# Weight buffers of an fp32r kernel: one tensor per slot, six offsets within 512 bytes

## What is computed

```python
for l in range(2):
    proj = rms_norm(x, norm_mix[l]) @ w_in[l]          # 1024 x 5120
    ...
    x = x + mixed @ w_out[l]                           # 1024 x 1024
    up = rms_norm(x, norm_ffn[l]) @ w_up[l]            # 1024 x 5632
    x = x + (silu(conv(up[..., :2816])) * up[..., 2816:]) @ w_down[l]
proj = rmsnorm(x, norm_mix_w) @ w_in_2                 # 1024 x 3080
...
x = x + mix @ w_out_2
u = relu(rmsnorm(x, norm_mlp_w) @ w_ff1)               # 1024 x 4096
x = x + (u * u) @ w_ff2
return rmsnorm(x, final_norm_w)
```

## Time and profile before

| | |
|---|---|
| median of three runs | 1057.65 us (1056.1 to 1057.9) |
| profiled execution | 1055.63 us |
| its span, first to last instruction | 1053.9 us |
| mean granted TensorE clock | 0.998 of 2.4 GHz |
| instructions | 20016 |

### The profile page before, as it was taken

How to read it: one execution, slowest core, us unless ns; L and a number is a source line. 1 busy time by engine, 2 the same in 40 slices (tenths; PEclk the granted TensorE clock), 3 DMA queues, 4 the chain that set the end, 5 groups by cost and what they waited for, 6 DMA issues and landing times.

```text
span 1053.9 us, 20016 instructions
## 1 busy us (share of the span) xinstructions
PE 1039.0 (99%) x8398; PEld 984.3 (93%) x8398; DVE 720.2 (68%) x1217; ACT 572.9 (54%) x791; POOL 287.1 (27%) x179
## 2 busy tenths in 40 slices
PE   8999999999999999999999999999899999999997
PEld 7999998999999899999999989998899999899996
DVE  5762248887687775322878967877887779666663
ACT  6454466655355645445665635566548865343443
POOL 0376665100000137666640000013300035101120
PEclk9999999999999999999999999999999999999999
DMA  9644445565654764444456576446432157664841
GB/s 310 200 161 150 160 162 160 160 219 162 223 197 126 223 212 160 137 148 153 158 166 208 160 233 201 143 139 220 121 117 86 61 181 229 190 210 129 260 162 40
DMA packets 169705, 180.11 MB, mean 171 GB/s; under 512 B 4240, under 2 KB 166416, under 8 KB 169488
## 3 DMA queue, kind: packets, MB, share of 16 engines
q1 hardware_dynamic: 169616, 178.84, 53.0%
HBM read 177.78 MB, written 1.05 MB: 170 GB/s over the span
## 4 chain that ended last, share of the span: by engine, by line
PE 84%; DVE 7%; ACT 4%; POOL 2%; issue 2%; DMA 1%; SPq 0%; POOLq 0%; ACTq 0%; DVEq 0%
PE psum L679 83%; DVE sb_w_lo L1861 2%; POOL sb_w_lo L2614 1%; ACT sb_scratch L1329 1%; ACT sb_w_hi L1329 1%; DVE sb_xg_lo L1845 1%; DVE psum L1845 1%; POOL sb_scratch L2654 1%; DMA sb_raw<-in_w_ff 1%; DMA sb_raw<-in_w_in 1%; PE psum L906 1%; DVE sb_hid_both L1936 0%; DVE sb_xt L1879 0%; DVE sb_scratch L1845 0%; DVE sb_xt L1877 0%
## 5 line engine op out<-in xcount | busy, mean ns | idle before, releaser
L1329 ACT ACTIVATE sb_w_hi<-sb_raw 128x2048 fp32r<-128x2048 f32 (+3 forms) x185 | 318.4, 1726 | 163.5 <-PE psum L679 99.0
L679 PE MATMUL psum<-sb_xg_hi,sb_w_hi 128*128 128x256 f32 x1656 | 401.8, 283 | 0.1
L679 PE MATMUL psum<-sb_xg_lo,sb_w_hi 128*128 128x256 f32 x1656 | 396.7, 279 | 0.0
L1861 DVE TENSOR_TENSOR sb_w_lo<-sb_raw,sb_w_hi 128x2048 fp32r<-128x2048 f32 (+3 forms) x150 | 305.9, 2042 | 104.7 <-ACT sb_w_hi L1329 103.8
L679 PEld LDWEIGHTS psum<-sb_xg_hi,sb_w_hi 128*128 128x128 f32 x1656 | 310.3, 187 | 3.3 <-DVE sb_xg_lo L1845 0.8
L679 PEld LDWEIGHTS psum<-sb_xg_lo,sb_w_hi 128*128 128x128 f32 x1656 | 310.7, 188 | 0.3
L679 PE MATMUL psum<-sb_xg_hi,sb_w_lo 128*128 128x256 f32 x1656 | 228.3, 280 | 0.1
L679 PE MATMUL psum<-sb_hid_both,sb_w_hi 128*128 128x512 f32 (+1 forms) x912 | 210.5, 364 | 1.3 <-DVE sb_xt L1874 0.6
L679 PEld LDWEIGHTS psum<-sb_xg_hi,sb_w_lo 128*128 128x128 f32 x1656 | 207.9, 187 | 1.0 <-DVE sb_w_lo L1861 0.3
L2614 POOL TENSOR_TENSOR sb_w_lo<-sb_raw,sb_w_hi 128x2048 fp32r<-128x2048 f32 (+1 forms) x34 | 156.0, 4595 | 107.3 <-ACT sb_w_hi L1329 97.9
L679 PEld LDWEIGHTS psum<-sb_hid_both,sb_w_hi 128*128 128x128 f32 x912 | 148.7, 188 | 23.0 <-DVE sb_hid_both L1936 1.2
(11 more groups left out here) (172 smaller groups left out, 987.3 us busy)
## 6 DMA issues: line engine op xcount, KB each, us to landing
sb_raw<-in_w_in SPq DMA_DIRECT2D x51, 1024.0 KB, 5.3
sb_raw<-in_w_up SPq DMA_DIRECT2D x44, 1024.0 KB, 5.1
sb_raw<-in_w_ff SPq DMA_DIRECT2D x21, 1024.0 KB, 5.7
sb_raw<-in_w_down SPq DMA_DIRECT2D x16, 768.0 KB, 4.8
sb_raw<-in_w_down SPq DMA_DIRECT2D x16, 640.0 KB, 4.4
sb_raw<-in_w_out SPq DMA_DIRECT2D x8, 1024.0 KB, 5.2
sb_raw<-in_w_ff SPq DMA_DIRECT2D x8, 768.0 KB, 4.5
sb_raw<-in_w_ff SPq DMA_DIRECT2D x8, 640.0 KB, 4.5
```

The source lines that it names most:

```text
L679: return nc.tensor.matmul(ps, lhsT, rhs, start=start, stop=stop, skip_group_check=True)
L1329: return nc.scalar.activation(out_, in_, func, **kw)
L1861: v.tensor_tensor(part(w_lo, s), part(raw, s), part(w_hi, s).bitcast(F32), ALU.subtract)\
```

## The change

The three tensors become nine, one for each slot and part, and five small tensors that nothing uses lie between them: before `w_hi1` 72 columns, before `w_hi2` 16, before `w_lo0` 120, before `w_lo1` 24 and before `w_lo2` 32, of 4 bytes each. `part` picks the tensor of the slot.

```diff
-        raw = sb("raw", SLOTS * SLAB)
-        w_hi = sb("w_hi", SLOTS * SLAB, F32R)
-        w_lo = sb("w_lo", SLOTS * SLAB, F32R)
+        def slots(name, before, dt=F32):
+            bufs = []
+            for i, gap in enumerate(before):
+                if gap:
+                    sb(f"before_{name}{i}", gap)
+                bufs.append(sb(f"{name}{i}", SLAB, dt))
+            return bufs
+
+        raw = slots("raw", (0, 0, 0))
+        w_hi = slots("w_hi", (0, 72, 16), F32R)
+        w_lo = slots("w_lo", (120, 24, 32), F32R)
...
         def part(buf, s):
-            i = s.n % SLOTS
-            return buf[:, i * SLAB:i * SLAB + s.chunks * s.cols]
+            return buf[s.n % SLOTS][:, 0:s.chunks * s.cols]
```

## The result

| | before | after |
|---|---|---|
| median of three runs, us | 1057.65 | 1064.26 (1061.48 to 1065.77) |
| profiled execution, us | 1055.63 | 1064.26 |
| its span, us | 1053.9 | 1062.5 |
| mean granted clock, of 2.4 GHz | 0.998 | 0.996 |

The changed kernel is slower: ratio 1.0057, interval 1.0034 to 1.0081. The forecast was no change; the time is inside its range, but the sign is that of the slower rival.

The account below looks back on a forecast made before the run. The prediction took PE's matmul count times its start-to-start step as the bound, apparently limited by the streaming operand. Transfers 0, splits 0 and matmuls 0 left the median at 1057.6 us, with a range from 1047 to 1066.

Parts of the forecast that it names:

- slower rival: Weight load becomes the bound at new distances; matmul step rises to 118.3 ns, 7.8 us more, 1065.5 us; chance 0.28.
- The first two steps: PE's matmul count times step sets the time, nobody keeps it waiting; transfers and splits change by 0 us.
- I take 0: Main matmuls: moving the stationary operand of 4872 matmuls costs nothing; bounds 16.1 us upward, 32.6 us downward.
- matmuls 0: Term of the sum for PE's matmuls: the new buffer distances change their time by 0 us.
- v: Matmuls of 256 columns with roles changed, weights streaming: 24 take 2.84 us, 118.3 ns each against the usual 116.7.
- vd: Matmuls with a stride of two in the stationary operand: 11 take 1.32 us, 120.0 ns each.
- the prediction's own test: Prediction is wrong if the matmul step differs by over 0.4 ns in the mean, or PE waits for a split.
- faster rival: Equal offsets cause a clash within the 116.7 ns step; two buffers put right give 1047 us, five 1025; chance 0.31.
- 2.84 or 2.88 us in the slabs of one slot alone: Sign in 24 matmuls of a projection slab: 2.80 us confirms the forecast's step, these longer times name a hurtful distance.
- whatever happens to the load: Sign in the 512-column stretches: they stay at 233.3 ns; if they shorten, the stream was not the limit.

Follow-up runs that it names:

- all0: Changed kernel with all six weight buffers at distance 0 from the activations (modulo 512 bytes): 1071.01 us, ratio 1.0128 to the kernel before.
- all64: Changed kernel with all six weight buffers at distance 64 from the activations: 1050.20 us, ratio 0.9931 to the kernel before; built again, 1050.28 us.
- sweep_a: Changed kernel with high buffers at distances 96, 160, 192 and low ones at 288, 320, 352: 1062.57 us, one run.
- all192: Changed kernel with all six weight buffers at distance 192 from the activations: 1056.11 us, ratio 0.9992 to the kernel before.
- all448: Changed kernel with all six weight buffers at distance 448 from the activations: 1059.09 us, one run.
- all80: Changed kernel with all six weight buffers at distance 80 from the activations: 1065.61 us, one run.
- hi1_at64: Changed kernel with only the high buffer of slot 1 moved, from distance 0 to 64: 1061.0 us, ratio 1.0034 to the kernel before.

## Why the prediction failed

**The first two steps hold.** PE's step sets the time, nobody keeps PE waiting, and transfers and splits cost 0 us: 1912, 2311 and 4735 ns, idle time 0.0 to 0.2 us before the main groups. Both also hold in all0 and all64, where DVE, ACT and POOL stay within 2 us while PE moves by 24.5 us.

**The step that failed** is "I take 0": "A limit in the stream does not care where the stationary operand lies." It rested on 512 columns taking twice 256 and on equal steps at 224 and -224. From it came the term "matmuls 0" of the sum, where 7.2 us are measured. Both equalities were read in one layout only. In all0 the narrow step is 119.75 ns and the wide one 231.43, and the wide one with streaming weights 226.9; in all64 they are 115.24, 232.6 and 229.1. Twice the narrow step is then 239.5 and 230.5: the factor of two was a coincidence of the layout before. One equality cannot show what a thing is limited by when the setting in which it holds was never varied. The rows that spoke the other way stood in the prediction: v at 118.3, vd at 120.0, a stretch at the usual distance at 117.9. The first of them was the distance's: in v the weights stream, so the stationary operand lies at -224, which is 288, and weights at distance 288 in sweep_a step by 118.5 ns; in all192 and all448, at 320 and 64, v goes down to 113.6. vd does not follow: 119.7 to 120.9 ns at all distances but one (117.8 in all80), so its stride is the likelier cause there. By the prediction's own test, 0.4 ns in the mean, 118.09 against 116.87 ns refutes it.

**The slower rival** had the right place and nearly the right price. Its first suspect, high slot 1 at distance 0, is the worst of the six, 119.50 ns, and hi1_at64 shows that the cost goes when it alone is moved. It took v's level for all five moved buffers, 118.3 ns and 7.8 us; measured are 116.47 to 119.50 ns and 7.2 us by steps, 6.6 us between the medians, 1064.26 against its 1065.5. That the sum comes so near is partly luck: the five buffers went by -0.4, 1.5, 1.5, 2.2 and 2.7 ns, not by 1.6 each, and the medians hold the clock's and the waits' share as well. That the load is what ends later, it named as mechanism; the trace does not split load and stream in time, so this stays argued. What is shown is that the two operands' distance does it.

**The faster rival** was no idle one, but its cause is refuted: equal offsets do not make the clash, since all64 has all six equal and is fast. What it hoped for is there at the right distance, 113.3 ns on all64's short level. The change gives that distance to one of its five buffers only, and in the mixed layout this buffer gains 0.4 ns (116.47), not the 1.6 of all64 (115.24); the other four get slower. Its forecast for five buffers put right, 1025, needed 110 ns, a difference read from starts rounded to 0.01 us. No run held a step below 113.3 ns; the lowest median is 1047.91.

**The page against the trace.** The prediction set two sections of the Trainium skill against each other. The 109.2 ns of TensorE: Matmul & The Clock Gate, section "Back-to-back issue gap", are not reached by any run of fp32r operands here: the shortest held level is 113.3 ns. The section gives its formula for an isolated matmul and says that pairs of load and matmul are spaced by both; these are such pairs, and the prediction should have said so. The separate ports of SBUF — State Buffer, section "Who interferes with whom", would let the step be the same wherever the operands lie; the trace disagrees, 119.75 ns at distance 0 and 115.24 at 64 with all else alike.

**The profile's signs.** "2.84 or 2.88 us in the slabs of one slot alone names the distance that hurts; 2.7 us names one that helps" worked in part: 2.86 at high slot 1 and 2.77 at the first tile of slot 2, but 2.85 at its second tile. The 512-column step, which should have stayed at 233.3 "whatever happens to the load", went to 228.6 in part of the last stage, which says by the prediction's own test that the limit was not the stream alone.

## What to carry to other kernels

Where TensorE's step sets the time, the place of the stationary operand against the streaming one is a tuning parameter: here the medians go from 1047.9 to 1071.0 us, 2.2%, with nothing changed in the instructions but addresses. Vary it with a small unused tensor ahead of the activations, the same for all buffers at once, read the distance of starts between two tiles in the timeline, and repeat the measurement, since a distance can hold two levels. Do not give each slot an offset of its own: the good distance is a property of the pair, so every buffer wants the same one, and in a mixed layout the good one gave less (116.5 ns in the changed kernel, 115.2 in all64). Which distance is good here holds for 256 columns; 512 columns want another.

## What was unexpected of the hardware

- The narrow matmul's step takes values between 113.3 and 120.0 ns, by the distance of its two operands. The short level was seen only at distances 128 bytes apart (64, 192, 320, 448), most at 64 and 320, and not 16 bytes beside 64 (118.7 and 117.9 ns).
- At those distances two levels, 113.3 and about 117.8 ns, are held for whole stretches, and the same program can take the one or the other in the same stretch.
- Matmuls of 512 columns go another way than the narrow ones: 229.0 and 229.1 ns where the stationary weights lie at 192 and 448, 232.6 and 232.5 at 64 and 320, and with streaming weights 226.9 at distance 0, where the narrow ones are slowest.
- Distances 256 bytes apart behave alike in these runs; distances 128 bytes apart share levels at most.
- In the same wait of about 3.2 us the granted clock fell for 6.8 us in one execution (after 2.3 us of idle PE), and not at all in another.

Open are: what chooses between the two levels where a stretch begins, how a buffer's neighbours change its step in a mixed layout (the 512-column one above all), and what it is inside the chip that makes the distance of the two operands count. No run here reaches those.
